# Three instead of two tiles' threshold searches on ScalarE in the attention stage, and the sink exponentials in groups of four

## The chip, the cores and the metric

The kernel runs on one core of a Trainium2 chip. The metric is the device time of one execution in microseconds. Three runs of the kernel before took 5094.94, 5096.12 and 5097.05 us; the median is 5096.12 us. Times of single instructions below come from one profiled execution. The engines are named as in the profile: PE is TensorE (matmuls and transposes), PEld its weight loads, DVE is VectorE, ACT is ScalarE, POOL is GpSimd, SP is SyncE, which here only issues DMAs.

## The reference, cut to what matters

One step of a hybrid attention layer on a prompt of 4096 rows (32 tiles of 128) and a small sample batch. Each row has eight heads of kind A (sliding window, with a learned sink per head) and eight of kind B (attention to the 256 keys that an indexer scores highest):

```
# A: softmax with a sink
m = jnp.maximum(jnp.max(s, axis=-1, keepdims=True), sk)
p = jnp.exp(s - m)
w = p / (jnp.sum(p, axis=-1, keepdims=True) + jnp.exp(sk - m))
# B: the 256 keys of highest indexer score, then attention to them
r = jax.nn.relu(jnp.einsum('bqhe,ble->bqhl', qi, ki_all).astype(jnp.float32))
score = jnp.einsum('bqhl,bqh->bql', r, wi.astype(jnp.float32))
_, idx = lax.top_k(score, topk)
s = jnp.where(valid[:, :, None, None, :], s + bias, -jnp.inf)
w = jax.nn.softmax(s, axis=-1)
```

The top-256 choice is made per row by a search for the 256th highest score: 32 counts of how many of the row's scores lie above a candidate, each halving the interval, and then a mask over the keys.

## The kernel before, in words

Three stages run one after another. Stage one (to about 2456 us) goes through the 32 prompt tiles and the sample tile: projections on PE, their evacuation on ACT, the indexer's scores on PE, ACT (relu) and POOL (weighing and adding, L908 to L913). For tile `a` the scores fill one of three row buffers of SBUF. The search of an even tile runs on ACT (`search` at L782, its full-width counts are L807), that of an odd tile on DVE (counts at L1043). Between the tests each engine does the rest of its own stage work. Where it does that is set by a planner that was run when the program was built: `act_us`, `dve_us` and `step_us` estimate how long a step takes, `search_times` places each test, and `advance` issues the background work that the plan has due by then. After a search DVE writes the mask: `choose_act` for a tile found on ACT (L989 to L999) and `choose` (L969 to L980), with one scan over the whole row (L972).

Tiles 30 and 31 aren't searched in stage one (`SEARCHED = TILES - 2`). Their scores go to DRAM (`late`). Stage two, the attention, goes through the tiles again. Tile t has six jobs (n = 6t + k): jobs k = 0 and 1 handle the A heads, four each, in two steps; jobs k = 2 to 5 handle two B heads each, in ceil((t+1)/4) steps of up to four key blocks ("wide steps"). In a step PE transposes the probabilities of two heads into PSUM (L1589), computes a piece of later scores (L1573), and applies the step before (L1618). ACT copies one head's transpose to SBUF (L1768), DVE the other's (L1945). PE's next transposes wait for both copies. After its copy, ACT has the exponentials that `PLAN` puts there (L1670), and then late-search items; DVE has mask additions and maxima (L1834).

The searches of tiles 30 and 31 ride in stage two (`LATE_SPANS = ((3, 18, 19), (20, 28, 29))`: first tile, last tile, closing tile). `late_search` on ACT splits a search into 161 items: the 32 counts have four items each (one per 1024 columns, L1703), and one item per count has the small operations that end it (L1685). They are spread evenly over the wide steps of the span. `late_close` on DVE has 23 items in the closing tile, among them a scan over the whole row in one instruction (L1912). SP loads the row (`load_late`, L1495) before the span and copies the mask from `late_mask` when its tile is due (L1468, L1469). The tile's sink exponentials are one ACT operation per head, after that head's exponential (L1656).

Of the kernel before, what the change touches and what calls it, by code (L numbers as in the profile page):

```python
# [127 lines left out]
RELU_GAP = 1.8  # L128
BIG = float(2 ** 100)
TESTS = 32  # L130
SEARCHED = TILES - 2
LATE_TILES = tuple(range(SEARCHED, TILES))


# [1126 lines left out]
def exp_pieces(n):  # L1261

    t, k = divmod(n, 6)
    if k < 2:
        pieces = [("exp", n, a_place(g, h)) for g in range(2) for h in range(2)]
        return [x for p in pieces for x in (p, ("sink", n, p[2]))]
    width = (t + 1) * P
    return [("exp", n, 2 * (c // (2 * STEP)) + h) for c in range(0, width, 2 * STEP) for h in range(2)]

# [23 lines left out]


QUARTER = 1024
LATE_SPANS = {1: ((3, 27, 28),), 2: ((3, 18, 19), (20, 28, 29))}[len(LATE_TILES)]


def wide_steps(first, last):
# [31 lines left out]
def stage_two(nc, rel_bias, sink_a, eye, qk_t, gates, values, chosen, late, ramp, mixed, a_k_prompt, a_v_prompt):  # L1331
    with ExitStack() as ctx:
        def sb(name, shape, dt=F32):
            return ctx.enter_context(nc.sbuf_tensor(name, shape, dt))

        def sem(name):
            return ctx.enter_context(nc.semaphore(name))
# [38 lines left out]
        a_sums = sb("a_sums", [P, HEADS])  # L1376
        b_sums = sb("b_sums", [P, 2, HEADS, 4])
        lsink = sb("lsink", [P, HEADS])
        total = sb("total", [P, HEADS])
        rinv = sb("rinv", [P, HEADS])  # L1380
        bank = ctx.enter_context(nc.psum_tensor("bank2", [P, 8 * STEP], F32))
# [34 lines left out]
        s_lfound = sem("late_found")  # L1416
        s_lmask = sem("late_mask_ready")
        s_lact = sem("late_act_ticks")
        block = ctx.enter_context(nc.Block())

        @block.sync
        def _(sp):
# [38 lines left out]
            def load_mask(t):  # L1461
                c = (t - 2) // 4
                far, near = (c + 1) * STEP, (t - 1) * P
                sp.wait_ge(s_used, units_through(6 * t - 7))
                sp.wait_ge(s_near, t - 1)
                if t in LATE_TILES:
                    sp.wait_ge(s_lmask, LATE_TILES.index(t) + 1)
                    sp.dma_start(mask[t % 2][:, 0:near], late_mask[:, 0:near]).then_inc(s_m[t % 2], 16)  # L1468
                    sp.dma_start(mask[t % 2][:, near:near + NEAR], late_mask[:, near:near + NEAR]).then_inc(s_m[t % 2], 16)  # L1469
                    return  # L1470
                sp.dma_start(mask[t % 2][:, 0:near], chosen[t, :, 0:near]).then_inc(s_m[t % 2], 16)
                sp.dma_start(mask[t % 2][:, near:near + NEAR], chosen[t, :, far:far + NEAR]).then_inc(s_m[t % 2], 16)
# [18 lines left out]
            def load_late(i):  # L1491
# [2 lines left out]
                width = (LATE_TILES[i] + 1) * P  # L1494
                sp.dma_start(late_row[:, 0:width], late[i, :, 0:width]).then_inc(s_lrow, 16)  # L1495

            load_late(0)
            for t in range(TILES + 1):
                if t >= 1:
                    sp.wait_ge(s_used, mixed_by(t - 1, 1))  # L1500
                    sp.dma_start(mixed[t - 1, :, STEP:2 * STEP], mixT[1][:, :]).then_inc(s_store[1], 16)
                if t in [close + 1 for _, _, close in LATE_SPANS[:-1]]:
                    load_late([close + 1 for _, _, close in LATE_SPANS].index(t) + 1)
                if t == TILES:
                    continue
                if t >= 1 and t + 1 < TILES:
                    load_qa(t + 1)
                    load_values(t + 1)
                    load_mask(t + 1)
                    load_q(t + 1)  # L1510
                sp.wait_ge(s_used, mixed_by(t, 0))
                sp.dma_start(mixed[t, :, 0:STEP], mixT[0][:, :]).then_inc(s_store[0], 16)
                if t + 1 < TILES:
                    sp.wait_ge(s_gp, 2 * t + 2)
                    sp.dma_start(gate[:, :], gates[t + 1]).then_inc(s_gate, 16)
# [133 lines left out]
        def _(act):  # L1649
            def exponential(kind, n, i):  # L1650
# [1 line left out]
                t, k = divmod(n, 6)  # L1652
                act.wait_ge(s_top, TOP_AT[n] + 1)
                if kind == "sink":
                    h = a_head(k, i)
                    act.activation(lsink[:, h:h + 1], sink[:, h:h + 1], ACT.Exp, bias=top_a[:, k, i:i + 1]).then_inc(s_sink, 1)  # L1656
                    return
                if k < 2:
                    if t:
# [121 lines left out]
        def _(dve):  # L1781
# [17 lines left out]
            def use(n, j):  # L1799
# [5 lines left out]
                if k < 2:  # L1805
# [11 lines left out]
                    dve.wait_ge(s_dve, m)  # L1817
                    if t:
                        dve.wait_ge(s_exp, exps_of_job(n - 6))
                        dve.wait_ge(s_sink, HEADS * t)  # L1820
                    dve.tensor_scalar(top_a[:, k, :], part_a[:, :], -1.0, None, ALU.mult).then_inc(s_top, 1)
                    return
                parts = [(i, p) for i, p in enumerate(biased_parts(n)) if c_in(p[0], *score_units(n)[j])]
# [25 lines left out]
            def scale_gate(t, b):  # L1849

                dve.wait_ge(s_gate, 16 * (t + 1))
                if b == 0:
                    dve.wait_ge(s_sink, HEADS * (t + 1))
                    dve.wait_ge(s_exp, max(exps_of_job(6 * t), exps_of_job(6 * t + 1)))
                    m = tick(dve.tensor_tensor(total[:, :], a_sums[:, :], lsink[:, :], ALU.add))
                else:
                    dve.wait_ge(s_exp, max(exps_of_job(6 * t + k) for k in range(2, 6)))
                    m = tick(dve.tensor_reduce(total[:, :], b_sums[:, t % 2, :, 0:-(-(t + 1) // 8)], AX.X, ALU.add))
# [18 lines left out]
            def late_close():  # L1877

                over, left, value, low, step, more = (l_pick[:, i:i + 1] for i in range(6))
                for i, a in enumerate(LATE_TILES):  # L1880
# [18 lines left out]
                    yield  # L1899
                    for q, (c, n) in enumerate(parts):  # L1900
                        if i:
                            dve.wait_ge(s_m[LATE_TILES[i - 1] % 2], 32 * (LATE_TILES[i - 1] // 2))
                        dve.wait_ge(s_dve, tick.n)
                        tick(dve.tensor_scalar(late_mask[:, c:c + n], late_row[:, c:c + n], value, -BIG, ALU.is_le, ALU.mult))
                        yield
# [628 lines left out]
```

## Time and profile before

| what | us |
|---|---|
| median of three runs | 5096.12 |
| the profiled execution | 5096.76 |
| its span, first to last instruction | 5095.0 |
| stage two begins (first DMA issue) | 2456.42 |
| stage two ends (POOL's first work of stage three) | 4495.34 |
| busy over the span: PE, DVE, ACT, POOL | 4347.4 (85%), 3499.8 (69%), 3443.3 (68%), 1619.9 (32%) |

The page, whose first part the last row repeats, gives each engine's busy time over the whole span. A busy PE isn't PE at its peak, since matmul ends are modelled; a wait is given by what released it. A row of the view by windows gives, for one stretch, its length and the busy time of PE, PEld, DVE, ACT and POOL, each with its number of instructions, then PE's granted clock as a share of full speed, the DMA engines' busy share and GB/s. The boundaries of the tile windows are the starts of POOL's `near_bias` operations (L1540, one a tile). The operation of tile t runs when the scores of tile t-1 are used up, which is about half a tile ahead of tile t's first job.

### The profile page before, as it was taken

The page shows a single profiled execution, that of the slowest core. Times are in us where ns is not written, and L with a number is a line of the kernel's source. Part 1 is how long each engine was busy: PE and PEld are TensorE (multiplying, and loading weights), DVE is VectorE, ACT ScalarE, POOL GpSimd, SP SyncE. Part 2 cuts the span into 40 slices and gives each one's busy share as a digit, 9 for nine tenths or more (in the row PEclk, how much of TensorE's full clock was granted, in tenths as well). Part 3 has the DMA queues.
Part 4 walks back from the last instruction along what each step waited for, and adds up shares of the span by engine and source line. Part 5 has one row for each costly group of instructions (what it writes and reads, how often), then busy time and mean ns, then how long its engine had stood idle before and what let it go on. Part 6 is the DMA issues. An engine that isn't in the chain of part 4 may idle for free. (4 is left out here: it accounts for less than half of the span.)

```text
span 5095.0 us, 78325 instructions
## 1 busy us (share of the span) xinstructions
PE 4347.4 (85%) x26505; PEld 2718.1 (53%) x26505; DVE 3499.8 (69%) x6644; ACT 3443.3 (68%) x6887; POOL 1619.9 (32%) x1358
## 2 busy tenths in 40 slices
PE   6777888777677786767689999989999999989999
PEld 3344444434343343434366777767777777754444
DVE  1277779888797898989477777787777778625111
ACT  1588888888787798872488888858788885520100
POOL 1345566667557757777210000000000000000000
PEclk8888889888788898978799999999999999999999
DMA  5211111100010111101421111011010010044422
GB/s 143 70 44 45 38 39 40 37 35 28 33 42 33 37 45 38 36 32 48 157 72 58 44 51 40 28 54 41 25 42 25 28 40 26 10 126 132 117 93 103
DMA packets 201975, 276.98 MB, mean 54 GB/s; under 512 B 50496, under 2 KB 134176, under 8 KB 201056
## 3 DMA queue, kind: packets, MB, share of 16 engines
q1 hardware_dynamic: 198624, 271.81, 16.9%
q8 instruction: 220, 3.60, 0.3%
q14 instruction: 171, 1.40, 0.1%
q10 hardware_dynamic: 2960, 0.17, 0.0%
HBM read 156.73 MB, written 114.16 MB: 53 GB/s over the span
## 5 line engine op out<-in xcount | busy, mean ns | idle before, releaser
L596 PE MATMUL bank<-w,x 128*128 128x512 f32 (+1 forms) x2848 | 1258.6, 598 | 19.2 <-DVE w L941 12.8
L1043 DVE TENSOR_SCALAR_CACHE_REDUCE ties<-score,cand 128x512 int8<-128x512 f32 (+13 forms) x448 | 1110.6, 2479 | 122.1 <-POOL score L917 106.7
L596 PEld LDWEIGHTS bank<-w,x 128*128 128x128 f32 x2848 | 576.9, 206 | 608.6 <-issue 549.7
L807 ACT ACTIVATE act_junk<-score,a_cand,a_sign 128x384 int8<-128x384 f32 (+13 forms) x420 | 879.4, 2094 | 14.0
L614 PE MATMUL bank<-kiT,qi 128*128 128x512 f32 (+3 forms) x1136 | 396.5, 489 | 450.5 <-ACT relu L737 244.9
L1834 DVE CUSTOM_DVE_ANT_0 row<-bank,mask 128x512 f32<-128x512 f32 (+3 forms) x1024 | 622.6, 639 | 181.6 <-PE bank L1573 180.3
L1540 POOL TENSOR_TENSOR near_bias<-table,mask 128x2048 f32<-128x2048 f32 (+1 forms) x32 | 129.5, 4047 | 1767.8 <-DVE part L1834 1751.4
L1768 ACT ACTIVATE pT<-bank 128x512 f32<-128x512 f32 (+2 forms) x704 | 368.4, 523 | 428.5 <-PE bank L1589 426.6
L1670 ACT ACTIVATE row<-row,top 128x1024 f32<-128x1024 f32 (+7 forms) x640 | 632.9, 990 | 4.0 <-DVE top L1847 4.0
L1573 PE MATMUL bank<-kT,qb 64*128 64x256 f32 (+1 forms) x4352 | 609.6, 397 | 9.0 <-DVE part L1834 5.6
L1589 PE MATMUL bank<-ident,row 128*128 128x128 f32 x4224 | 594.6, 281 | 26.4 <-DVE pT L1945 19.6
L1945 DVE COPY pT<-bank 128x512 f32<-128x512 f32 (+2 forms) x704 | 425.2, 604 | 255.8 <-PE bank L1589 254.2
L1618 PE MATMUL bank<-pT,v 128*64 128x128 f32 x8448 | 590.0, 280 | 0.0
L913 POOL TENSOR_TENSOR score<-score,relu 128x512 f32<-128x512 f32 (+3 forms) x426 | 560.3, 1315 | 33.4
L614 PEld LDWEIGHTS bank<-kiT,qi 128*128 128x128 f32 x1136 | 237.6, 232 | 578.3 <-ACT relu L737 307.0
L1618 PEld LDWEIGHTS bank<-pT,v 128*64 128x64 f32 x8448 | 450.9, 137 | 171.1 <-issue 163.7
L910 POOL TENSOR_TENSOR relu<-relu,weight 128x512 f32<-128x512 f32 (+3 forms) x426 | 499.3, 1172 | 76.9 <-ACT relu L737 76.7
L1589 PEld LDWEIGHTS bank<-ident,row 128*128 128x128 f32 x4224 | 453.1, 141 | 132.2 <-issue 97.0
L737 ACT ACTIVATE relu<-bank 128x512 f32<-128x512 f32 (+3 forms) x568 | 297.7, 554 | 252.1 <-POOL score L913 177.0
L2290 PE MATMUL bank<-wo,mix_in 128*128 128x512 f32 x1024 | 450.9, 599 | 0.0
L1573 PEld LDWEIGHTS bank<-kT,qb 64*128 64x128 f32 x4352 | 380.3, 187 | 125.5 <-issue 72.1
L908 POOL TENSOR_TENSOR score<-relu,weight 128x512 f32<-128x512 f32 (+3 forms) x142 | 164.6, 1159 | 651.4 <-issue 527.9
(255 smaller groups left out, 4900.1 us busy)
## 6 DMA issues: line engine op xcount, KB each, us to landing
qk_t<-ring SPq DMA_DIRECT2D x66, 256.0 KB, 2.0
gates<-ring SPq DMA_DIRECT2D x66, 256.0 KB, 2.0
gate<-gates SPq DMA_DIRECT2D x33, 512.0 KB, 3.4
out<-x_in SPq DMA_DIRECT2D x33, 512.0 KB, 2.9
x<-in_x_prompt SPq DMA_DIRECT2D x32, 512.0 KB, 3.7
mixed<-mixT SPq DMA_DIRECT2D x64, 256.0 KB, 2.0
mix_in<-mixed SPq DMA_DIRECT2D x32, 512.0 KB, 4.3
x_in<-in_x_prompt SPq DMA_DIRECT2D x32, 512.0 KB, 3.8
```

The source lines that it names most:

```text
L596: ins = pe.matmul(p_bank[n % 2][:, 0:n1 - n0], held[:, c * P:(c + 1) * P], w[:, c, n0:n1], start=(c == 0), stop=(c == KC - 1))
L614: ins = pe.matmul(s_bank[at % 4][:, 0:n], qi[:, part, h * P:(h + 1) * P], kiT[:, c:c + n], start=(part == 0), stop=(part == 1))
L807: tick(act.activation(junk, row, ACT.Sign, bias=c, scale=back, accum_out=a_sum[:, :]))
L910: k = tick(pool.tensor_tensor(r, r, weighs, ALU.mult))
L913: pool.tensor_tensor(to, to, r, ALU.add).then_inc(s_pa, 1)
L1043: n = tick(dve.tensor_scalar(ties[:, 0:width], row, c.bitcast(F32), 0.0, ALU.is_ge, ALU.add, accum_out=counts[:, i:i + 1]))
L1573: ins = pe.matmul(s[:, h * STEP + c0:h * STEP + c0 + m], qb[t % 2][half, g, :], kT[half, c + c0:c + c0 + m], start=True, stop=True)
L1589: ins = pe.transpose(t_bank[h][:, b * P:(b + 1) * P], held, ident[:, :])
L1618: ins = pe.matmul(oT[0 if k < 2 else 1][half * HD:(half + 1) * HD, col:col + P], value, pT[h][at % 2][:, b * P:(b + 1) * P], start=first, ...
L1670: act.activation(at, at, ACT.Exp, bias=bias, accum_out=out).then_inc(s_exp, 1)
L1834: ins = dve.tensor_tensor_reduce(row[k % 2][:, h, c0:c0 + w0], s[:, h * STEP + c0 - c:h * STEP + c0 - c + w0], more, 1.0, PAD, ALU.add, AL ...
L2290: ins = pe.matmul(y_bank[k % 2], held, w[:, c, i * STEP:(i + 1) * STEP], start=(c == 0), stop=(c == KC - 1))
```

## The change

`SEARCHED` is `TILES - 3`: tile 29 is no longer searched by DVE in stage one but by ACT in stage two. The spans become tiles 2 to 14 (closing in 15), 16 to 22 (closing in 23) and 24 to 28 (closing in 29). The mask of a late tile goes to DRAM with one DMA after its closing tile (`store_late`) and is loaded from there. The sink exponentials of a job become one ACT operation on four columns; DVE computes its argument in one added operation per A job.

```diff
-SEARCHED = TILES - 2
+SEARCHED = TILES - 3
...
         pieces = [("exp", n, a_place(g, h)) for g in range(2) for h in range(2)]
-        return [x for p in pieces for x in (p, ("sink", n, p[2]))]
+        return pieces[0:2] + [("sink", n, 0)] + pieces[2:4]
...
-LATE_SPANS = {1: ((3, 27, 28),), 2: ((3, 18, 19), (20, 28, 29))}[len(LATE_TILES)]
+LATE_SPANS = ((2, 14, 15), (16, 22, 23), (24, 28, 29))
...
                 if t in LATE_TILES:
-                    sp.wait_ge(s_lmask, LATE_TILES.index(t) + 1)
-                    sp.dma_start(mask[t % 2][:, 0:near], late_mask[:, 0:near]).then_inc(s_m[t % 2], 16)
-                    sp.dma_start(mask[t % 2][:, near:near + NEAR], late_mask[:, near:near + NEAR]).then_inc(s_m[t % 2], 16)
+                    sp.wait_ge(s_lstore, 16 * (LATE_TILES.index(t) + 1))
+                    sp.dma_start(mask[t % 2][:, 0:near], chosen[t, :, 0:near]).then_inc(s_m[t % 2], 16)
+                    sp.dma_start(mask[t % 2][:, near:near + NEAR], chosen[t, :, near:near + NEAR]).then_inc(s_m[t % 2], 16)
...
+            def store_late(i):
+                a = LATE_TILES[i]
+                sp.wait_ge(s_lmask, i + 1)
+                sp.dma_start(chosen[a, :, 0:(a + 1) * P], late_mask[:, 0:(a + 1) * P]).then_inc(s_lstore, 16)
...
-                if t in [close + 1 for _, _, close in LATE_SPANS[:-1]]:
-                    load_late([close + 1 for _, _, close in LATE_SPANS].index(t) + 1)
+                for i, (_, _, close) in enumerate(LATE_SPANS):
+                    if t == close + 1:
+                        store_late(i)
+                        if i + 1 < len(LATE_SPANS):
+                            load_late(i + 1)
...
                 if kind == "sink":
-                    h = a_head(k, i)
-                    act.activation(lsink[:, h:h + 1], sink[:, h:h + 1], ACT.Exp, bias=top_a[:, k, i:i + 1]).then_inc(s_sink, 1)
+                    act.activation(lsink[:, :].rearrange("p (v g) -> p v g", v=KVH)[:, :, 2 * k:2 * k + 2],
+                                   sink_d[:, k, :].rearrange("p (v g) -> p v g", v=KVH), ACT.Exp).then_inc(s_sink, 1)
...
+                    tick(dve.tensor_tensor(sink_d[:, k, :].rearrange("p (v g) -> p v g", v=KVH),
+                                           sink[:, :].rearrange("p (v g) -> p v g", v=KVH)[:, :, 2 * k:2 * k + 2],
+                                           part_a[:, :].rearrange("p (v g) -> p v g", v=KVH), ALU.subtract))
+                    dve.wait_ge(s_dve, tick.n)
                     dve.tensor_scalar(top_a[:, k, :], part_a[:, :], -1.0, None, ALU.mult).then_inc(s_top, 1)
```

What moves on the engines, at the places of which the prediction speaks. First DVE at the end of stage one, before: the head sums of step 31 are followed by three-operation tests of tile 29 (L1043, L1047, L1050), and the choice for tile 28 (L989 on) comes after four of them.

```order
L946 TENSOR_TENSOR ties<-proj 128x1280
L950 TENSOR_REDUCE head_sum<-ties 128x20
L1047 TENSOR_SCALAR flag<-counts 128x1
L1050 TENSOR_SCALAR cand<-flag,cand 128x1
L1043 TENSOR_SCALAR ties,counts<-score,cand 128x3840
```

And the same place now, where the choice for tile 28 stands directly behind the head sums:

```order
L946 TENSOR_TENSOR ties<-proj 128x1280
L950 TENSOR_REDUCE head_sum<-ties 128x20
L989 TENSOR_SCALAR pick<-a_found 128x1
L991 SCALAR_TENSOR_TENSOR pick<-a_found,pick 128x1
L993 TENSOR_SCALAR ties,pick<-score,pick 128x3712
```

All 32 tests of tile 29, and the choice for tile 29 with its scan, are gone from DVE; the choice for tile 28 still stands ahead of the split of step 31's indexer keys (L956, L961).

Second, ACT in job k = 4 of tile 24 of stage two, before (pT is the copy, L1670 an exponential, L1703 a late count, L1685 the small operations that end a count):

```order
L1768 ACTIVATE pT_0<-bank 128x512
L1703 ACTIVATE late_junk,l_sums<-late_row,l_cand,l_sign 128x1024
L1768 ACTIVATE pT_1<-bank 128x512
L1670 ACTIVATE row,b_sums<-row,top 128x1024 x2
L1685 ACTIVATE l_sums,l_sum<-l_sums 128x4
L1685 ACTIVATE l_sign<-l_sum,l_sign 128x1
L1685 ACTIVATE l_cand<-l_sign,l_cand,l_step 128x1
L1768 ACTIVATE pT_0<-bank 128x512
L1670 ACTIVATE row,b_sums<-row,top 128x1024
L1768 ACTIVATE pT_1<-bank 128x512
L1670 ACTIVATE row,b_sums<-row,top 128x1024
L1703 ACTIVATE late_junk,l_sums<-late_row,l_cand,l_sign 128x1024
```

The same job from its fourth step on now (the lines are ten higher: L1778, L1680, L1713, L1695):

```order
L1778 ACTIVATE pT_1<-bank 128x512
L1680 ACTIVATE row,b_sums<-row,top 128x1024
L1713 ACTIVATE late_junk,l_sums<-late_row,l_cand,l_sign 128x1024
L1778 ACTIVATE pT_0<-bank 128x512
L1680 ACTIVATE row,b_sums<-row,top 128x1024 x2
L1713 ACTIVATE late_junk,l_sums<-late_row,l_cand,l_sign 128x1024 x2
L1778 ACTIVATE pT_1<-bank 128x512
L1680 ACTIVATE row,b_sums<-row,top 128x128
L1713 ACTIVATE late_junk,l_sums<-late_row,l_cand,l_sign 128x1024
```

Every wide step now has a late item, and some have two, where before some had none.

Third, SP where a row of late scores is loaded, before (the start of tile 20):

```order
L1501 DMA mixed<-mixT 128x512
L1495 DMA late_row<-late 128x4096
L1442 DMA qa<-qk_t 128x512
L1444 DMA ka<-qk_t 128x2x128
L1457 DMA va<-values 128x2x128
```

Now (the start of tile 24; the start of tile 16 is like it), with the store of the mask ahead of the load:

```order
L1508 DMA mixed<-mixT 128x512
L1502 DMA chosen<-late_mask 128x3968
L1497 DMA late_row<-late 128x4096
L1444 DMA qa<-qk_t 128x512
L1446 DMA ka<-qk_t 128x2x128
```

The load of the next row is behind a store of 1 MB in the same queue.

## Rows read from the trace of the kernel before

**Rows 1.** By windows: the new spans' stretches, then tile windows around the first closing.
```profile
3718.60:4186.30 467.70, 464.63 (x4720) 354.95 (x4718) 330.14 (x903) 386.49 (x847) 20.42 (x5) 1.00 0.10 31
3109.40:3634.80 525.40, 504.58 (x5042) 382.78 (x5042) 391.76 (x1051) 413.89 (x950) 28.98 (x7) 0.99 0.12 39
2523.50:3048.90 525.40, 491.07 (x4795) 365.47 (x4796) 391.52 (x1179) 434.77 (x1115) 53.12 (x13) 0.99 0.18 55
...
3275.70:3345.90 70.20, 69.15 (x701) 52.87 (x699) 58.23 (x161) 50.55 (x121) 4.08 (x1) 1.00 0.12 38
3345.90:3435.90 90.00, 77.24 (x747) 58.40 (x745) 72.95 (x172) 53.39 (x120) 4.46 (x1) 0.92 0.15 53
3435.90:3513.60 77.70, 76.50 (x767) 57.32 (x762) 54.80 (x145) 65.31 (x150) 4.09 (x1) 1.00 0.10 35
```
**Rows 2.** By windows over stage two, sums of L1703 alone and L1685 alone.
```profile
sum 2020.70, ACT 334.58; mean ACT 10.46
sum 2020.70, ACT 70.01; mean ACT 2.19
```
**Rows 3.** Waits of PE in two stretches: 3718.6 to 4186.3, then 2523.5 to 3048.9.
```profile
PE bank L1589 <- ACT pT L1768: 2.7, 11, 0.5
...
PE bank L1589 <- ACT pT L1768: 13.5, 30, 1.2
```
**Rows 4.** Timeline of ACT, then PE, in a wide step (start, length, idle before).
```profile
3856.75 1.23 ACT L1703 ACTIVATE late_junk<-late_row,l_cand,l_sign 128x1024 int8<-128x1024 f32 x1
3857.98 0.58 ACT L1768 ACTIVATE pT<-bank 128x512 f32<-128x512 f32 x1
3858.46 1.14 ACT L1670 ACTIVATE row<-row,top 128x1024 f32<-128x1024 f32 x1
...
3856.42 1.09 PE L1589 MATMUL bank<-ident,row 128*128 128x128 f32 x8
3859.53 1.09 PE L1589 MATMUL bank<-ident,row 128*128 128x128 f32 x8
```
**Rows 5.** Timeline around both closings: DVE, PE, PE, ACT, PE.
```profile
3357.94 8.42 DVE L1912 TENSOR_TENSOR_SCAN late_row<-late_tie 128x3968 f32<-128x3968 int8 x1
...
3367.27 1.11 PE L1589 MATMUL bank<-ident,row 128*128 128x128 f32 x4 [8.23 <-DVE pT L1945]
...
4259.29 1.11 PE L1589 MATMUL bank<-ident,row 128*128 128x128 f32 x4 [5.42 <-DVE pT L1945]
...
3404.40 1.15 ACT L1703 ACTIVATE late_junk<-late_row,l_const 128x1024 int8<-128x1024 f32 x1 [3.68 <-DMA late_row<-late]
...
3406.18 1.53 PE L1589 MATMUL bank<-ident,row 128*128 128x128 f32 x8 [2.02 <-ACT pT L1768]
```
**Rows 6.** Timeline of the last step of stage one: ACT, DVE, PE, POOL.
```profile
2305.91 0.18 ACT L853 ACTIVATE a_found<-a_sign 128x1 f32<-128x1 f32 x1
...
2314.69 0.21 DVE L989 TENSOR_SCALAR pick<-a_found 128x1 f32<-128x1 f32 x1
2399.22 8.88 DVE L972 TENSOR_TENSOR_SCAN score<-ties 128x3840 f32<-128x3840 int8 x1
...
2341.91 3.59 PE L614 MATMUL bank<-kiT,qi 128*128 128x512 f32 x8 [13.48 <-DVE kiT L961]
2424.97 9.85 PE L596 MATMUL bank<-w,x 128*128 128x512 f32 x16 [6.33 <-ACT ring L700]
2434.66 7.03 PE L596 MATMUL bank<-w,x_later 128*128 128x512 f32 x16
...
2400.05 8.88 POOL L910 TENSOR_TENSOR relu<-relu,weight 128x512 f32<-128x512 f32 x1
...
2420.28 1.04 POOL L910 TENSOR_TENSOR relu<-relu,weight 128x512 f32<-128x512 f32 x1
```
**Rows 7.** By lines: the sink exponentials; DMA issues: the mask store of stage one.
```profile
L1656 ACT ACTIVATE lsink<-sink,top_a 128x1 f32<-128x1 f32 x256 | 73.1, 285 | 0.0
...
chosen<-mask SPq DMA_DIRECT2D x1, 896.0 KB, 3.6
```

More of the change, by code:

```diff
@@ L1378, in stage_two @@
         lsink = sb("lsink", [P, HEADS])
+        sink_d = sb("sink_d", [P, 2, GROUP])
         total = sb("total", [P, HEADS])
@@ L1418, in stage_two @@
         s_lact = sem("late_act_ticks")
+        s_lstore = sem("late_mask_stored")
         block = ctx.enter_context(nc.Block())
@@ L1819, in use @@
                         dve.wait_ge(s_exp, exps_of_job(n - 6))
-                        dve.wait_ge(s_sink, HEADS * t)
+                        dve.wait_ge(s_sink, 2 * t)
+                    tick(dve.tensor_tensor(sink_d[:, k, :].rearrange("p (v g) -> p v g", v=KVH),
+                                           sink[:, :].rearrange("p (v g) -> p v g", v=KVH)[:, :, 2 * k:2 * k + 2],
+                                           part_a[:, :].rearrange("p (v g) -> p v g", v=KVH), ALU.subtract))
+                    dve.wait_ge(s_dve, tick.n)
                     dve.tensor_scalar(top_a[:, k, :], part_a[:, :], -1.0, None, ALU.mult).then_inc(s_top, 1)
@@ L1852, in scale_gate @@
                 if b == 0:
-                    dve.wait_ge(s_sink, HEADS * (t + 1))
+                    dve.wait_ge(s_sink, 2 * (t + 1))
                     dve.wait_ge(s_exp, max(exps_of_job(6 * t), exps_of_job(6 * t + 1)))
@@ L1901, in late_close @@
                         if i:
-                            dve.wait_ge(s_m[LATE_TILES[i - 1] % 2], 32 * (LATE_TILES[i - 1] // 2))
+                            dve.wait_ge(s_lstore, 16 * i)
                         dve.wait_ge(s_dve, tick.n)
```

## The prediction

> **What bounds the kernel now.** The page's busy times (in the table above) put PE first, with DVE and ACT close together behind it. That average mixes stages, so the windows come next, over the three stretches in which the new spans will lie. (Tile t's jobs run from the middle of its window to the middle of the next one.) Between 3718.6 and 4186.3 us, tiles 24 to 28, PE is busy for 464.6 of 467.7 us, ACT for 386.5 and DVE for 330.1; in tiles 16 to 22 ACT has 413.9 of 525.4 us, in tiles 2 to 14 434.8 of 525.4 [rows 1]. PE paces the attention. The view of waits says how near ACT is to it: PE waited for ACT's copy for 2.7 us in the first of these stretches and for 13.5 us in the last [rows 3]. The reader should see that ACT's idle time, 81 us in tiles 24 to 28, is the room from which a denser search would have to be paid. Last, the timelines: of one wide step, of the two closings, and of the end of stage one.
>
> **Stage one, what goes.** DVE loses the 32 tests and the choice of tile 29. DVE's busy time there is worth nothing as such; what counts is who waited for it. Two places do.
> 1. PE stood idle for 13.48 us until 2341.91, for the split of step 31's indexer keys on DVE [rows 6]. The split stands behind the choice for tile 28 in both orders. ACT had the threshold at 2305.91 + 0.18 = 2306.1, but DVE took it up at 2314.69 [rows 6], after tests of tile 29. In the new order four relus and a copy come before ACT's last operation of the search, some 1.4 us. DVE starts at 2307.5: 7.2 us earlier, and PE with it.
> 2. The choice of tile 29 stalled POOL. While DVE's scan took 8.88 us, a POOL multiplication that takes 1.04 behind it took 8.88 as well [rows 6], and its neighbours beside DVE's other wide operations were stretched too. PE's last scores lost about 4 us by that, the gate projection at 2424.97 then waited 6.33 us, and it took 9.85 us where the same 16 matmuls took 7.03 behind it [rows 6]. Without the stretch POOL is done before PE asks: 4 + 6.3 + 2.8 = 13 us.
>
> Together 7.2 + 13 = 20 us, and 21 with the last waits between PE and ACT. The tail behind it (ring copies, stores, the last row of late scores) stays. Bounds: 8, if only the first place counts, and 28, if PE also waits out the multiplication's excess, 8.88 - 1.04. I take -21.
>
> **Stage two, the density on ACT.** A search has 161 items and 404.6 / 2 = 202 us of ACT [rows 2], 1.26 us an item with overlapped reads in it; one count of 1024 columns holds ACT for 3857.98 - 3856.75 = 1.23 us [rows 4]. Before, an item came to 0.84 of the wide steps of tiles 3 to 18 and 0.70 in tiles 20 to 28. The new spans have 123, 145 and 139 steps for 161 items each: 1.31, 1.11 and 1.16 a step. In tiles 24 to 28 ACT goes from 97 items to 161. That adds 64 x 1.26 = 81 us; the sink operations give back about 6. ACT's busy time comes to 461 of 467.7 us, 98.5%. In tiles 16 to 22 it comes to some 94%, in tiles 2 to 14 to 93%, but unevenly.
>
> Averages hide the jobs. PE's wide step takes 3859.53 - 3856.42 = 3.11 us. ACT's copy holds it for 3858.46 - 3857.98 = 0.48 us, an exponential of 1024 columns 1.13 [rows 4]. In a job k = 3 or 4 of tile 24 PE has six full steps and one of a single block: 6 x 3.11 + 1.0 = 19.7 us. ACT has copies of 3.2 us, six wide and two narrow exponentials of 7.6, and 7 x 1.16 items of 1.22 = 9.9: 20.7 us. Before it was 16.7. k = 5 has four A exponentials more and one item step fewer: 21.3. So three jobs in a row are 1.0 to 1.6 us too long on ACT. Jobs 0 and 1 are short on PE and full of exponentials on ACT; only k = 2 has room. ACT can lag by about 1.8 us before PE's next transposes wait (they need the copy that could have been done that much earlier). Hence 3 to 4 us are lost at tile 24, 3 at 25 and 26, 2 at 27, 3 at 28: 15, less 3 that are lost today: +13. The same sum for tile 16 (PE 13.4, ACT 14.2) and on gives +11; for tile 12 (PE 3 x 3.11 + 1.0 = 10.3; ACT 1.7 + 3.9 + 6.1 = 11.7, before 9.6), tile 8 and their neighbours +15, and +6 for the small tiles 2 to 7. Sum +45. Bounds: 0, since each average leaves some idle time, and 75, if the steps with two items stall as well. I take +45, nearer to the job sums, which are rows.
>
> The Trainium skill (Perfetto Trace Analysis, Identifying the Most-Contended Engine) judges TensorE by its weight loads and the other engines by occupancy, and takes the highest for the bound. Here PEld has 354.95 us, ACT 386.49 [rows 1]: by that page ACT is the most contended already, although PE hardly waits for it [rows 3]. Taken alone the rule would make the third stretch as long as ACT's 461 us, so no longer than now, and the sum 13 us less.
>
> **A third closing.** The tile window with the first closing took 90.0 us between neighbours of 70.2 and 77.7 [rows 1]: 16 too many. PE waited 8.23 us in it behind DVE's 8.42 us scan [rows 5]; about 3.6 belong to the next item. The second had a wait of 5.42 [rows 5]: 7 with the slow steps behind it. DVE's closing work is 58.23 + 72.95 less twice some 52 = 27 us. Tile 15 is short: 16 wide steps of 3.11 us and some 10 for its A steps, 60. DVE needs three quarters of that for itself, as in the stretch before it (391.5 of 525.4 [rows 1]), 45, and 45 + 27 is 12 too many; I price it at 15, as the first closing also cost more than its overflow. Tile 23 lies between, 10. New 15 + 10 + 7 = 32, old 12.4 + 7: +12.5, bounds +5 (a scan must stall once more) and +25.
>
> **A second wait for a row.** ACT waited 3.68 us for the late row's load at tile 20, and PE 2.02 behind it [rows 5], then ran slowly for a step (1.53 us for what takes 1.09 [rows 4, 5], at a granted clock of 0.92 over the window [rows 1]). 3.6 us in all. Now this happens at tiles 16 and 24, each time behind a 1 MB store; the 896 KB store of a mask took 3.6 us to land [rows 7]. 2 x 7.2 - 3.6 = +11, bounds +4 (no queueing) and +16. What is queued behind the waiting count on ACT is the copies, and PE waits for those.
>
> **Sinks.** 192 of 256 operations of 285 ns [rows 7] go; each held ACT for about 0.18 us: 35 us, most of it idle time or already in the sums above. 64 added DVE operations of about 0.17 us, each with a wait, lie in front of the maxima; DVE's idle time hides them, and they'd cost 0.3 us apiece without it. I take -3, bounds -15 and +5. The mask's way through DRAM for tiles 29 to 31 is asked for most of a tile ahead: 0.
>
> **Sum.** -21 + 45 + 12.5 + 11 - 3 = +44.5 on the profiled execution's 5096.76 us: 5141.3. The median is 0.6 lower: 5141.
>
> **Rivals.**
> (a) ACT absorbs the density: its idle time (81 us in the third stretch) takes the items and PE's slack takes the jitter. For it: PE's wait for ACT is 0.6% of that stretch today. Against it: the job sums above. Then density +8, closing +8, row +8, sinks -4, stage one -21: 5096, no change.
> (b) Stage one gives its upper bound and the rest its lower ones, one mechanism: PE's clocked work in stage two has more slack than its modelled busy time shows, so nothing shorter than a scan reaches it: -28 + 0 + 5 + 4 - 10 = -29: 5068, faster. It decides this way if PE's waits for ACT's copy stay under 30 us in stage two. For it: only modelled ends; against it: the 13.5 us of waits at today's lower density [rows 3].
> (c) ACT becomes the bound outright, and steps with two items stall PE every time: density +100: 5196.
> (d) The plan doesn't do what it says, since stage one ends where it did (another wait, of ACT for its ring, takes the place): stage one -5, the rest as forecast: 5157.
>
> **Chances.** Forecast 0.58, (a) 0.16, (b) 0.10, (c) 0.06, (d) 0.10. 10 us, 0.2%, is about what a measurement tells from no change. Faster: (b) and the lower part of (a), 0.14; same: the rest of (a) and a little of the forecast, 0.12; slower 0.74. The range takes in the forecast's bounds and most of (a) and (d): 5102 to 5172.
>
> **What would show it.** Stage two's first DMA issue near 2435 instead of 2456; no long POOL operation beside a scan at stage one's end; PE's waits for ACT's copy in stage two at 60 us or more, most in tiles 8 to 16 and 24 to 28; ACT idle under 10 us in the third stretch, which then takes 480 us; three windows with a PE wait of 5 to 8 us behind a scan; two waits for the late row of about 7 us. The forecast is wrong if PE's waits for ACT stay as they are, or if stage one ends at 2450 or later.

## The result, and the profile after

The changed kernel took 5116.79 us (median of five runs, 5113.98 to 5121.81), the kernel before 5094.94 beside it: ratio 1.0045, 95% interval 1.0032 to 1.0059. So it is slower, by 22 us, which is just under half of the 44.5 forecast. Its profiled execution took 5115.78 us, with a span of 5114.0.

The first part of the page, which answers to the last row of the table before:

```profile
PE 4348.6 (85%) x26505; PEld 2720.7 (53%) x26505; DVE 3366.5 (66%) x6604; ACT 3578.2 (70%) x7099; POOL 1611.3 (32%) x1359
```

DVE lost 133 us, ACT gained 135, PE's work is unchanged. Neither sum says anything about the 22 us.

**Stage one.** Timeline of its end, four engines and SP's first DMA of stage two:

```profile
2305.48 0.21 DVE L989 TENSOR_SCALAR pick<-a_found 128x1 f32<-128x1 f32 x1 [20.69 <-ACT a_found L853]
2334.99 3.78 PE L614 MATMUL bank<-kiT,qi 128*128 128x512 f32 x8 [9.64 <-DVE kiT L961]
2400.38 1.04 POOL L910 TENSOR_TENSOR relu<-relu,weight 128x512 f32<-128x512 f32 x1
2412.79 7.03 PE L596 MATMUL bank<-w,x_later 128*128 128x512 f32 x16
2434.62 0.34 SPq L1425 DMA_DIRECT2D ident<-in_eye  x1
```

DVE takes up the threshold as soon as ACT has it (2305.48, before 2314.69), PE's wait for the split ends 6.9 us earlier, POOL's multiplications at 2400 take 1.04 us each where one took 8.88 [rows 6], and the last projections follow one another at 7.03. Stage two starts at 2434.62 instead of 2456.42: 21.8 us earlier, 21 forecast. Of these, 14.9 lie behind the split, and they repeat: stage two begins 114.2 to 114.6 us after the split in the profiles of all five kernels that search tile 29 in stage one, and 99.0 to 99.7 after it in the nine others. The split's own place repeats less well. It comes at 2341.7 to 2344.6 in the five and at 2329.3 to 2338.3 in the nine, so the 6.9 is one profile's figure, and a difference of some us between two kernels can be stage one's.

**Stage two** took 2038.9 us before (2456.42 to 4495.34) and 2081.3 after (2434.62 to 4515.96): 42.4 more, 65.5 forecast. The windows between `near_bias` operations (L1550 now) place it. The first three rows are those of windows 16, 24 and 30 before. Then come the same windows now, which are those of the first closing, the second and the third, and last the stretch in which the jobs of tiles 25 to 28 run:

```profile
3077.96:3140.68 62.72, 60.67 (x619) 45.88 (x617) 45.26 (x139) 52.25 (x125) 4.08 (x2) 1.00 0.13 41
3675.90:3761.31 85.41, 84.88 (x875) 65.27 (x873) 61.29 (x179) 70.49 (x156) 4.09 (x2) 1.00 0.10 33
4237.37:4351.05 113.68, 106.73 (x1061) 81.23 (x1061) 92.54 (x214) 60.90 (x126) 4.47 (x2) 0.97 0.08 27
...
3063.78:3147.78 84.00, 65.89 (x616) 48.66 (x614) 65.59 (x154) 47.05 (x112) 4.46 (x1) 0.90 0.18 66
3670.27:3774.03 103.76, 90.02 (x875) 67.91 (x873) 80.98 (x194) 67.27 (x149) 4.46 (x1) 0.95 0.16 57
4257.92:4371.85 113.93, 107.03 (x1061) 81.50 (x1061) 92.88 (x216) 60.00 (x120) 4.46 (x1) 0.97 0.11 36
3818.00:4206.00 388.00, 381.62 (x3872) 291.24 (x3870) 270.38 (x746) 367.99 (x801) 16.36 (x4) 1.00 0.09 30
```

Numbered by their place, windows 16 and 24 are 21.3 and 18.4 us longer than before, window 20 (90.0 before [rows 1]) is 16.9 shorter, window 30 the same: +23.0 for the closings and the row waits together, 23.5 forecast. The other 27 windows, from the first `near_bias` to the last, add 20.3, where density and sinks together were to add 42; the two ends of stage two are 0.9 shorter. The difference lies in the 27 windows and nowhere else. PE's waits in stage two, with the number and the longest, and ACT's for the late row:

```profile
PE bank L1599 <- ACT pT L1778: 42.4, 74, 5.7
PE bank L1599 <- DVE pT L1959: 40.6, 38, 6.6
...
ACT late_junk L1713 <- DMA late_row<-late: 11.6, 2, 7.0
```

Before, the first was 27.4 us in 77 waits. The timeline around window 16, DVE, PE, ACT, PE:

```profile
3071.18 8.16 DVE L1926 TENSOR_TENSOR_SCAN late_row<-late_tie 128x3840 f32<-128x3840 int8 x1
3080.25 1.11 PE L1599 MATMUL bank<-ident,row 128*128 128x128 f32 x4 [6.60 <-DVE pT L1959]
...
3121.03 1.15 ACT L1713 ACTIVATE late_junk<-late_row,l_const 128x1024 int8<-128x1024 f32 x1 [6.96 <-DMA late_row<-late]
3124.07 1.97 PE L1599 MATMUL bank<-ident,row 128*128 128x128 f32 x8 [5.71 <-ACT pT L1778]
```

Both kinds of wait were forecast: three waits of 5 to 8 us behind a scan, and two of about 7 for the row. PE waited 6.6, 5.4 and 5.4 us behind the three scans. ACT waited 7.0 us for the row at tile 16, but only 4.6 at tile 24; PE behind it 5.7 and 4.5.

### The profile page after: what moved, and what is told of

The parts are those of the page before. It is cut to its first block and busy times, and to the rows that moved or that the text cites. A ratio compares the mean times of both kernels' runs of the same rounds, so it can differ in the third digit from the quotient of the medians.

```text
span 5114.0 us, 78504 instructions
## 1 busy us (share of the span) xinstructions
PE 4348.6 (85%) x26505; PEld 2720.7 (53%) x26505; DVE 3366.5 (66%) x6604; ACT 3578.2 (70%) x7099; POOL 1611.3 (32%) x1359
## 3 DMA queue, kind: packets, MB, share of 16 engines
q1 hardware_dynamic: 199056, 277.80, 17.2%
## 5 line engine op out<-in xcount | busy, mean ns | idle before, releaser
L1043 DVE TENSOR_SCALAR_CACHE_REDUCE ties<-score,cand 128x512 int8<-128x512 f32 (+12 forms) x416 | 975.8, 2346 | 105.2 <-POOL score L917 90.8
L1550 POOL TENSOR_TENSOR near_bias<-table,mask 128x2048 f32<-128x2048 f32 (+1 forms) x32 | 129.9, 4059 | 1810.0 <-DVE part L1848 1794.3
L1680 ACT ACTIVATE row<-row,top 128x1024 f32<-128x1024 f32 (+7 forms) x640 | 633.5, 991 | 2.3 <-DVE top L1861 2.3
L1583 PE MATMUL bank<-kT,qb 64*128 64x256 f32 (+1 forms) x4352 | 611.1, 398 | 12.5 <-DVE part L1848 9.1
L1778 ACT ACTIVATE pT<-bank 128x512 f32<-128x512 f32 (+2 forms) x704 | 366.3, 520 | 323.6 <-PE bank L1599 322.4
L910 POOL TENSOR_TENSOR relu<-relu,weight 128x512 f32<-128x512 f32 (+3 forms) x426 | 488.6, 1147 | 76.2 <-ACT relu L737 75.9
L1713 ACT ACTIVATE late_junk<-late_row,l_cand,l_sign 128x1024 int8<-128x1024 f32 x360 | 434.4, 1207 | 2.0
```

What stands on the lines that cost most here:

```text
L910: k = tick(pool.tensor_tensor(r, r, weighs, ALU.mult))
L1043: n = tick(dve.tensor_scalar(ties[:, 0:width], row, c.bitcast(F32), 0.0, ALU.is_ge, ALU.add, accum_out=counts[:, i:i + 1]))
L1583: ins = pe.matmul(s[:, h * STEP + c0:h * STEP + c0 + m], qb[t % 2][half, g, :], kT[half, c + c0:c + c0 + m], start=True, stop=True)
L1680: act.activation(at, at, ACT.Exp, bias=bias, accum_out=out).then_inc(s_exp, 1)
```

## The experiments

Tile windows are compared with those of the kernel before, each in its own profile; "others" is the sum over the 27 windows besides 16, 20, 24 and 30. Each comes from one profiled execution, but where two kernels have the same code the windows agree well: others are +20.3 in the change, +20.5 in the run with the row load ahead and +18.1 in the one with the scan in pieces.

**Sinks alone** (the kernel before, with the change's sink exponentials and nothing else):

```diff
-        return [x for p in pieces for x in (p, ("sink", n, p[2]))]
+        return pieces[0:2] + [("sink", n, 0)] + pieces[2:4]
...
```

> Before, with the sink exponentials four columns at a time and the added DVE operation, nothing else. Theory A: -1 to -4 us, 5092, since ACT has idle time in nearly every tile. Theory B: -15 us or more, 5080.

5078.66 us, 0.997 (0.9959 to 0.9981). By the profile stage two ends 14.7 us earlier, and others are -14.3: nearly every window from 9 to 29 is 0.2 to 2.0 us shorter. PE's waits for ACT's copy fell from 27.4 to 12.8 us:

```profile
PE bank L1590 <- ACT pT L1769: 12.8, 45, 2.0
```

So the sinks are worth five times the 3 us of the forecast. The timeline of one A step shows where. Before (ACT, but for the last row):

```profile
2636.67 0.36 ACT L1768 ACTIVATE pT<-bank 128x256 f32<-128x256 f32 x1
...
2637.42 0.29 ACT L1656 ACTIVATE lsink<-sink,top_a 128x1 f32<-128x1 f32 x1
...
2638.10 0.29 ACT L1656 ACTIVATE lsink<-sink,top_a 128x1 f32<-128x1 f32 x1
2638.29 1.03 ACT L1670 ACTIVATE row<-row,top 128x896 f32<-128x896 f32 x1
...
2639.31 0.37 ACT L1768 ACTIVATE pT<-bank 128x256 f32<-128x256 f32 x1
...
2639.73 0.66 PE L1589 MATMUL bank<-ident,row_a 128*128 128x128 f32 x4 [0.83 <-ACT pT L1768]
```

And the same step of the changed kernel:

```profile
2616.70 0.37 ACT L1778 ACTIVATE pT<-bank 128x256 f32<-128x256 f32 x1
...
2617.95 1.03 ACT L1680 ACTIVATE row<-row,top 128x896 f32<-128x896 f32 x1
...
2618.98 0.36 ACT L1778 ACTIVATE pT<-bank 128x256 f32<-128x256 f32 x1
2619.39 0.66 PE L1599 MATMUL bank<-ident,row_a 128*128 128x128 f32 x4 [0.33 <-ACT pT L1778]
```

From copy to copy ACT needed 2.64 us and needs 2.28; PE's wait went from 0.83 to 0.33. In this step ACT paces PE, and its two sink operations, 0.19 us each from start to start, are paid in full. Of the 77 waits of PE for ACT's copy before, 53, with 21.8 of the 27.4 us, stood behind a step with sink operations (summed from the trace); in the changed kernel two do, with 1.7 us.

**Density alone** (the kernel before, its second search within tiles 20 to 24 instead of 28):

```diff
-LATE_SPANS = {1: ((3, 27, 28),), 2: ((3, 18, 19), (20, 28, 29))}[len(LATE_TILES)]
+LATE_SPANS = {1: ((3, 27, 28),), 2: ((3, 18, 19), (20, 24, 29))}[len(LATE_TILES)]
```

> Before, with one number changed: the search of tile 31 in tiles 20 to 24 instead of 20 to 28 (161 items over 119 wide steps, 1.35 a step instead of 0.70); closing tile and row load unchanged. It has the density alone. Theory A (ACT's lag is mostly absorbed; the change's third span, 1.16 a step, lost about 7 us in five tiles): +8 to +12 us, 5105. Theory B (each job's excess on ACT is lost, by the forecast's sums 1.3 + 1.3 + 2 us a tile): +20 us or more, 5115.

5131.58 us, 1.0074 (1.0061 to 1.0086). At 1.35 items a step the windows 21 to 25 grew by 8.0, 6.1, 4.8, 5.0 and 6.7 us, and PE's waits for ACT's copy doubled to 55.4 us. Density costs PE time, and ACT's idle time doesn't absorb it (rival (a)).

**Counts on quarter columns** (the change, each late count over a quarter of its columns; the thresholds of tiles 29 to 31 differ):

```diff
...
-late_tick(act.activation(late_junk[:, 0:n], late_row[:, c0:c0 + n], ACT.Sign
+late_tick(act.activation(late_junk[:, 0:n // 4], late_row[:, c0:c0 + n // 4], ACT.Sign
```

> The change, with each late count over a quarter of its columns only (256 of 1024; the threshold is then another, so the output differs). All items, waits, closings and row loads stay; ACT loses some 250 us of count time and is lighter than before the change. Theory A: the 20 us of density go and some 10 of the waits on ACT that were there before: 5117 - 30 = 5087. Theory B: the whole 45 and the 10: 5062.

5078.38 us, 0.9971 (0.9961 to 0.9982): 38 below the change. Others are -12.4, nearly those of the sinks alone, and the windows of closings stay (16 +21.9, 20 -17.2, 24 +18.1). With counts this short ACT has less late work than before the change, and the density's price is gone but for 2 us: it is the counts' length on ACT, not their number.

**The change with the old sinks** (one operation per head again, nothing else undone):

```diff
-        return pieces[0:2] + [("sink", n, 0)] + pieces[2:4]
+        return [x for p in pieces for x in (p, ("sink", n, p[2]))]
...
```

> The change with the sink exponentials as before (one ScalarE operation per head), nothing else undone. Theory A, terms add: the sinks alone took 14.7 us from the profiled end of the kernel before, so without them the change should stand 15 us higher, near 5132, some 37 over the kernel before, the extra spread over nearly every tile at about 1 us each. Rival B, the sinks' worth is larger here because the denser late items leave ScalarE no room: +20 or more, 5137 and above, with most of it in tiles 2 to 14 and 24 to 28. Rival C, the forecast's own -3: 5120, and the gain seen on the kernel before was something else.

5139.09 us, 1.0084 (1.0071 to 1.0098), so +44.1. PE waits 71.5 us for ACT's copy:

```profile
PE bank L1598 <- ACT pT L1777: 71.5, 119, 5.4
```

47.6 of it, in 76 waits, behind steps with sink operations. This is the run that settles the forecast. Others, by sinks and density:

| | density before | density of the change |
|---|---|---|
| one sink operation per head | 0 | +44.6 |
| four columns at a time | -14.3 | +20.3 |

Density costs 44.6 us with the old sinks and 34.6 with the new; the sinks give 14.3 at the old density and 24.3 at the new one. The two aren't additive by the windows (rival B of the expectation), and the 10 us between them are far more than the 2 us by which the runs with the same work in these windows differ. By the medians the sinks give 22.3 in the change and 15.2 alone; their intervals, 5 to 7 us each way for each kernel, don't separate the two, so the interaction rests on the windows.

**Without the third closing** (tile 29 isn't searched in stage two and takes tile 30's mask; the spans of before for tiles 30 and 31):

```diff
-LATE_SPANS = ((2, 14, 15), (16, 22, 23), (24, 28, 29))
+LATE_SPANS = ((3, 18, 19), (20, 28, 29))
...
```

> The change, but the search and closing of tile 29 are left out of stage two (its mask is that of tile 30, so the output differs), and tiles 30 and 31 have the spans of before: 3 to 18 closing in 19, 20 to 28 closing in 29. Both theories: stage one ends 22 us earlier, as in the trace of the changed kernel. Theory A (what the two traces' tile windows show: the density costs about 20, closings and row waits 23): 5095 - 22 - 1 (sinks) + 3 (mask store ahead of the row load) = 5075. Theory B (the density costs the 45 us of the forecast, and something that both kernels' windows hide, the sinks above all, gave 25 back): 5095 - 22 - 25 = 5048 to 5052.

5061.55 us, 0.9937 (0.9924 to 0.9949). That lies between the two theories (5075, and 5048 to 5052). Stage one's gain and the sinks' remain, -32 in all, though window 20, now with a store ahead of the row's load, is 2.6 longer. So the third search in stage two costs 5117 - 5062 = 55 us, for 22 in stage one.

**The closing scan in four pieces** of 1024 columns, items of their own:

```diff
-                    m = tick(dve.tensor_tensor_scan(row, tie, tie, 0.0, ALU.add, ALU.max))
+                    for q, (c, n) in enumerate(parts):
...
+                        m = tick(dve.tensor_tensor_scan(late_row[:, c:c + n], tie, tie, late_row[:, c - 1:c] if q else 0.0, ALU.add, ALU.max))
```

> The change, with the closing's whole-row scan on DVE cut into four scans of 1024 columns, each in an item of its own and started from the last column of the one before (same result). DVE's work stays within 1 us. Theory C (a closing costs because one instruction of 8.4 us holds PE's copies): the windows of tiles 16, 24 and 30 lose 4 to 6 us each, 5117 - 14 = 5103. Theory D (a closing costs because DVE has more work than the tile has time, the scan's length doesn't matter): tile 15's closing stays as it is (12 us too many there), the others lose 1 to 2 us each: 5113.

5117.12 us, 1.0042 (1.0029 to 1.0054): nothing. The longest wait of PE for DVE's copy fell from 6.6 to 3.5 us, but the sum stayed, and windows 16 and 24 are 84.4 and 103.9:

```profile
PE bank L1599 <- DVE pT L1963: 38.9, 43, 3.5
```

The wait behind the scan is where DVE's excess is paid, not its cause.

**Closings on quarter columns** (the wide operations of all three; the rest of each late mask stays zero):

```diff
-                    width, parts = (a + 1) * P, quarters(a)
+                    width, parts = (a + 1) * P // 4, [(c, n // 4) for c, n in quarters(a)]
...
```

> The change with each wide operation of the three closings (flags, mask, ties, scan, ranks, sum) on a quarter of its columns, the rest of the late masks being left at zero, so that the outputs of tiles 29 to 31 differ; the number of items, their places and waits are as in the change. Theory D, what a closing costs is the column work that VectorE has not the time for: the three windows lose most of their excess; without the second row wait tile 16's window was 76.8 us and tile 24's 98.2, with it 84.0 and 103.8, so they come to about 72 and 93 here, and tile 30's from 113.7 to near 107; total 5117 - 25 to 30 = near 5090. Rival E, the cost is in the number of dependent items and their fixed waits, or in the store and load behind them: the windows lose under 5 us each and the total stays above 5105.

5084.83 us, 0.998 (0.9972 to 0.9989): 32 less than the change. Windows 16, 24 and 30 lose 10.4, 9.5 and 8.2 us, 28.2 together. Windows 0 and 1 grow by 3.8, where the run has two memsets more at its start, and the rest stay; in its profile stage two began 4.6 us earlier, which isn't the closings'. The window of the first closing:

```profile
3061.73:3135.30 73.57, 64.89 (x619) 49.18 (x617) 52.32 (x154) 47.50 (x112) 4.09 (x2) 0.93 0.21 75
```

The number of DVE instructions is the same (154), its busy time 13.3 us less, the window 10.4. DVE's column work in too short a tile is the price, at some 9.4 us a closing; the number of items and the fixed waits between them are not.

**Spans 2 and 3 five steps later**, so that the row is there when ACT asks:

```diff
-    _steps = [(n, g) for n, g in wide_steps(_first, _last) if n % 6 != 5 or g < n_steps(n) - 1]
+    _steps = [(n, g) for n, g in wide_steps(_first, _last) if n % 6 != 5 or g < n_steps(n) - 1][0 if _first < 16 else 5:]
```

> The change, with the second and third span starting five wide steps later, so that ACT doesn't ask for the late row before it has landed (161 items over 140 and 134 steps). If the row's wait costs the 7 us each of the forecast, ACT's two waits (11.6 us in the changed kernel) go and 5117 - 14 + 2 (density) = 5105. The rival is that PE's lag absorbs most of the wait and the denser span gives it back: 5113 to 5117.

5105.07 us, 1.002 (1.0011 to 1.0029). No wait for the late row is left; window 16 is 76.8 and window 24 98.2, 7.2 and 5.5 less. The two row waits cost at most 12.7 us: the first late items leave these windows too, and others are 1.9 us longer.

**Row load ahead of the mask store**, otherwise the change:

```diff
-                        store_late(i)
                         if i + 1 < len(LATE_SPANS):
                             load_late(i + 1)
+                        store_late(i)
```

> The change, with the load of the next late row issued before the store of the mask instead of behind it. If the store ahead in the queue delays the load by the 3.6 us of the forecast: ACT's waits at tiles 16 and 24 fall from 11.6 us together to about 4 to 5, and the time by 6 to 7: 5110. The rival is that both transfers share the 16 DMA engines whatever their order: waits of 10 us or more, 5116.

5114.37 us, 1.0038 (1.0025 to 1.005), by its interval no different from the change. ACT's waits for the row went from 11.6 to 9.7 us, windows 16 and 24 are 83.4 and 104.0. By the traces the queue isn't what ACT waits for. Behind the store the two loads took 10.3 and 9.7 us from issue to landing, ahead of it 9.8 and 9.6, and with no store near them 9.0 (before, tile 20) and 8.8 (sinks alone); the store itself takes 5.3 ahead of the load and 11.4 and 11.5 behind it. A store ahead costs the load about 1 us, and most of the wait is the load's own length. Only starting the use later helps.

**Two late tiles with three of these edits** (the new sinks, the scan in pieces, the second span five steps later):

> Before (two late tiles, spans 3 to 18 and 20 to 28), with the sink exponentials four at a time, the scan in four parts, and the second span five wide steps later. By theory C: 5079 (sinks, measured) - 10 (two closings) - 3.6 (row wait) = 5065. By theory D: 5079 - 4 - 3.6 = 5072. Either is faster than before and after.

5075.78 us, 0.9963 (0.995 to 0.9975), 3 less than the sinks alone and short of both theories. Window 20 is 2.4 us shorter than before and only 1.4 shorter than with the sinks alone, although ACT's wait for the row there, 3.7 us, is gone. The closings are still paid.

**Closings spread over two tiles** (as the last, with the mask by way of DRAM; the lines are against those of the change):

```diff
...
-LATE_SPANS = ((2, 14, 15), (16, 22, 23), (24, 28, 29))
+LATE_SPANS = ((3, 17, 19), (20, 27, 29))
...
-    _steps, _many = wide_steps(_close, _close), 2 + 5 * len(quarters(_a)) + 1
+    _steps, _many = wide_steps(_close - 1, _close), 2 + 6 * len(quarters(_a))
...
```

> A version meant to beat both kernels: two late tiles (30, 31) as before, the sinks four columns at a time, the closing spread over two tiles (18 and 19; 28 and 29) instead of one, its scan in four pieces, the counts ending one tile earlier (tiles 3 to 17; 20 to 27), the second span five steps late, the mask by way of DRAM. If VectorE's overload in one tile is the price of a closing (Theory D), the windows of tiles 20 and 30 lose about 8 and 4 us against the version with closings of one tile (5075.8), and the denser counts give 3 us back: 5067. Rival E, fixed costs per item: no change, 5076 to 5080.

5056.1 us, 0.9924 (0.9911 to 0.9938): 39 below the kernel before, 61 below the change, and 11 below the 5067 expected. Windows of the first closing (19 and 20), and PE's waits in stage two:

```profile
3260.49:3331.58 71.09, 69.29 (x701) 52.84 (x699) 65.21 (x157) 41.60 (x93) 4.45 (x1) 1.00 0.12 37
3331.58:3407.86 76.28, 73.10 (x747) 55.62 (x745) 62.17 (x168) 48.58 (x108) 5.00 (x2) 1.00 0.21 76
```

```profile
PE bank L1599 <- DVE pT L1963: 18.3, 24, 2.0
PE bank L1599 <- ACT pT L1778: 11.3, 45, 0.7
```

Against [rows 1] the window of 90.0 us at a clock of 0.92 is one of 76.3 at 1.00; window 30 lost 9.4. Against the version before this one, with closings of one tile, windows 20 and 30 lost 11.3 and 9.9, where 8 and 4 were expected, and windows 19 and 29 grew by 1.9 and 0.6.

**Three late tiles with spread closings**, the scans in pieces and the row waits removed too:

```diff
-LATE_SPANS = ((2, 14, 15), (16, 22, 23), (24, 28, 29))
+LATE_SPANS = ((2, 13, 15), (16, 21, 23), (24, 27, 29))
...
```

> The change with its three closings spread over two tiles each, scans in four pieces, spans 2 and 3 begun five steps late, and the counts for that ending one tile earlier: tiles 2 to 13, 16 to 21, 24 to 27, 161 items on 108, 117 and 103 steps (1.49, 1.38 and 1.56 a step; the change has 1.31, 1.11, 1.16). Closings: three overloads of VectorE fall away, about 35 us less, and 12 of row waits. Density: worked out from the trace of before, ScalarE without late items is busy for some 211 of the 373 us of tiles 24 to 27 and some 245 of 450 in tiles 16 to 21; 161 items of 1.26 us make that 414 of 373 and 448 of 450. Theory, ScalarE becomes the bound outright where its sum exceeds PE's time: +41 in the third span, +5 to 15 in the second, +15 to 25 in the first, beside the change's own 38: near 5140. Rival, PE's lag tolerance and idle time elsewhere take most of it: 5090 or less, and three late tiles would be nearly as good as two.

5141.3 us, 1.0096 (1.0079 to 1.0113), as expected to 2 us, which is in part luck: by the windows the second span, 17 to 23 without 20, added 21.2 where 5 to 15 had been expected, and in this profile stage two began 5.8 us earlier than in the change's. The closings' windows are cheap now (16 +3.4, 20 -14.3, 24 +4.0, 30 -9.8), but others are +87.9, 44.5 of it in windows 25 to 29 where 41 had been worked out. Four windows of the third span, and PE's waits in them:

```profile
3769.30:4187.73 418.43, 380.66 (x3783) 289.31 (x3780) 271.18 (x747) 388.64 (x842) 16.32 (x5) 0.98 0.09 28
```

```profile
PE bank L1599 <- ACT pT L1778: 36.4, 38, 2.4
```

PE waited 36.4 us for ACT in this stretch, and yet ACT was busy for only 388.64 of 418.43 us, 93%: here an engine that hands work to and fro with PE set the pace before its busy time was full.

## Why the prediction was right in direction and wrong in size

| term | forecast | measured | from |
|---|---|---|---|
| stage one | -21 | -21.8 | start of stage two |
| density | +45 | +44.6 with the old sinks, +34.6 with the new | windows |
| third closing and second row wait | +23.5 | +23.0 | windows 16, 20, 24, 30 |
| sinks | -3 | -14.3 alone, -24.3 in the change | windows |

For the change as it is, -21.8 + 44.6 - 24.3 + 23.0 = +21.5, against +21.9 by the medians. Put the other way, with the interaction counted to the density, it is -21.8 + 34.6 - 14.3 + 23.0: the density was then 10 us too high in the forecast and the sinks 11 too low.

**The step that failed is the sinks term.** The prediction had the right 35 us of ACT's time, and called most of it idle time or already in the sums. For the kernel before that is half true: 14.3 of the 35 were paid. In the change 24.3 were. The job sums of the density credited the sinks with some 6 us in one span and were otherwise worked out for the old work. And the prediction itself called jobs 0 and 1 short on PE and full of exponentials on ACT: that is where the sink operations stand, between two copies, and in the step shown 0.19 us of ACT is 0.19 us of the kernel. The bound of -15 was too narrow for the change, since the denser items left those steps less slack. The trace of before held the answer: the prediction read how long PE waited for ACT, 13.5 us in one stretch [rows 3], and not behind which steps. Without this term it forecast +47.5, and the change with the old sinks measured +44.1.

**Stage one: right.** The last scores gave 14.9 us (13 and 1 forecast), and that figure repeats. No long POOL operation stands there any more. The split came 6.9 us earlier (7.2 forecast), which agrees better than one profile can show, since over the runs its place varies by 9 us. Rival (d) is out. No run takes the two places apart; they are read from the timelines.

**Density: right in sum if the old sinks are left in, wrong in its picture of ACT.** With the old sinks windows 25 to 29 added 13.6 us (13 forecast), 17 to 23 without 20 added 10.8 (11), 2 to 15 20.0 (21). The lag that PE tolerates was 1.8 us in the sums. It can be read in the changed kernel:

```profile
3861.63 1.09 PE L1599 MATMUL bank<-ident,row 128*128 128x128 f32 x8
3864.93 0.58 ACT L1778 ACTIVATE pT<-bank 128x512 f32<-128x512 f32 x1
3865.56 0.66 PE L1599 MATMUL bank<-ident,row 128*128 128x128 f32 x4 [0.74 <-ACT pT L1778]
```

The copy starts 3.30 us after the transposes, where 0.7 is usual, and PE waits 0.74: 3.30 - 0.7 - 0.74 = 1.86. Of the signs named for it one came: the third stretch, tiles 24 to 28, takes 481 us (480 forecast; its ends are matched by the count of PE's transposes), some of it the wait for the row at its start.

```profile
3726.30:4207.60 481.30, 467.15 (x4710) 355.50 (x4710) 331.13 (x913) 451.90 (x986) 20.43 (x5) 1.00 0.11 36
```

The others didn't. PE waited for ACT's copy for 42.4 us in stage two and not 60 or more, and 10.2 of that stood behind the late row; with the old sinks it was 71.5, so this sign failed with the sinks term. But ACT's idle time in the third stretch is 29 us and not under 10, and with the old sinks it was 30.5 of 488.7. PE lost time there although ACT wasn't full. Rivals (b), waits under 30 us, and (c), a density of 100, are out.

**Closing and row wait: right in sum, the row wait not in its cause.** The row waits cost at most 12.7 us. The forecast then took off 3.6 for the one of before, but with that one gone, and the scan in pieces, window 20 was only 1.4 shorter. So the second row wait is 9 to 11 us (11 forecast), and the rest, 12 to 14, the third closing (12.5). The forecast had each row wait made of 3.6 us as before and 3.6 of queueing behind the store. The store ahead cost the load about 1 us; the rest of the difference at tile 16 is that ACT asked for the row 3.4 us after the load was issued, where it was 5.3 in the kernel before. The agreement of the sum is in part luck. That DVE's column work and not the scan's length sets the price, as the prediction had priced it from its overflow, was shown by the quarter columns and the pieces.

**The rule on the most-contended engine** (the Trainium skill, Perfetto Trace Analysis, Identifying the Most-Contended Engine), weighed in the prediction, puts ACT first. In the changed kernel's inner windows ACT shows 367.99 us of 388.00 and PEld 291.24, and PE waited 4.2 us for ACT: the rule names the engine that would bind next, and the run with spread closings of three tiles is where it did.

**The sinks' own duration** agrees with the Trainium skill (ScalarE: Activation LUTs, What ACT_TABLE_LOAD costs): an operation whose bias is a pointer takes about 280 ns there and 0.83 ns more for each column, 285 here for one column [rows 7], and back-to-back operations overlap by about 93, as the 0.19 us between starts shows. What it costs the kernel no such figure tells.

## What to carry to other kernels

A small operation on an engine that hands work to and fro can cost nothing or its full length, by the step in which it stands: before pricing it by the engine's idle time, list the waits that end behind it, with what stood in the step. An edit's worth depends on what else is packed there, so price two edits of one engine together, or measure the corners. Work that overflows one short tile is better spread over two than cut into smaller instructions.

## What the runs showed that was not expected

- A closing was much cheaper once spread over two tiles: windows 20 and 30 are 13.7 and 9.4 us shorter than before, and the granted clock in window 20 was 1.00 instead of 0.92. PE's 747 matmuls are in that window both times; they are busy for 77.24 us at 0.92 and 73.10 at 1.00, so some 4 of the 13.7 us is PE's slower work and the rest is waiting. The idle time came first: PE stood still for the 8.23 us before 3367.27 [rows 5], and the clock went from 2.4 to 1.2 GHz within them, at 3362.3. It was back at 3372.6, with PE at work.
- A scan of 3840 columns on DVE took 8.16 us; pieces of 1024 took 2.29 to 2.35 us each. They saved PE nothing, although its longest wait halved.
- The three loads of late rows (1920, 1984 and 2048 KB) took 8.2, 10.3 and 9.7 us to land, the first without a store ahead of it; the 1 MB stores took 5.2 to 5.3. Over all runs a load without a store ahead took 8.2 to 10.3 us, one with a store ahead 9.5 to 10.8. Swapping store and load took 1.9 us off ACT's two waits together.
- In the profiles of the nine kernels with three tiles taken out of stage one, that stage ends anywhere between 2428.8 and 2438.0 us, at a granted clock of 0.865 to 0.860. Medians of two such kernels that differ by a few us may differ by that alone.
